# Feed-forward up projection by 7 block products in place of 8, inner tiles in parts of 4, 6, 6, 6

## The reference, cut to what matters

```
def swiglu(x, w_in, w_out):
    gate, up = jnp.split(x @ w_in, 2, axis=-1)
    return (jax.nn.silu(gate) * up) @ w_out
...
h = swiglu(rmsnorm(x, g[0]), lw['ffn_in'][0], lw['ffn_out'][0])
x = x + FFN_RES * rmsnorm(h, g[1])
```

## Time and profile before

| | us |
|---|---|
| median of 3 runs | 2804.49 (2799.52 to 2805.52) |
| the profiled execution, its span | 2804.8 |
| DVE busy | 1252.4 |
| ACT busy | 888.5 |
| POOL busy | 382.5 |

### The profile page before, as it was taken

How to read it: one execution, slowest core, us unless ns; L and a number is a source line. 1 busy time by engine, 2 the same in 40 slices (tenths; PEclk the granted TensorE clock), 3 DMA queues, 4 the chain that set the end, 5 groups by cost and what they waited for, 6 DMA issues and landing times.

```text
span 2804.8 us, 45262 instructions
## 1 busy us (share of the span) xinstructions
PE 2723.6 (97%) x18703; PEld 2610.5 (93%) x18703; DVE 1252.4 (45%) x1697; ACT 888.5 (32%) x1213; POOL 382.5 (14%) x350
## 2 busy tenths in 40 slices
PE   8999999999899999999999999999989999999999
PEld 8999999997679899999999999999966889999998
DVE  4332333647665633333363323345475746332333
ACT  4221123425543422122342212233164533221223
POOL 0110011102143110011101001110022430100110
PEclk9999999999999999999999999999999999999999
DMA  4223223320015222222322222142101152222222
GB/s 131 75 62 89 75 58 88 87 55 10 23 45 93 61 75 71 79 75 58 92 61 75 68 82 75 56 112 69 37 11 32 38 106 66 73 66 82 75 61 81
DMA packets 367939, 191.19 MB, mean 68 GB/s; under 512 B 36477, under 2 KB 363472, under 8 KB 367822
## 3 DMA queue, kind: packets, MB, share of 16 engines
q1 hardware_dynamic: 363822, 179.07, 23.8%
q0 software_dynamic: 4000, 10.47, 1.6%
HBM read 183.58 MB, written 5.93 MB: 68 GB/s over the span
## 4 chain that ended last, share of the span: by engine, by line
PE 88%; DVE 5%; ACT 3%; issue 2%; DMA 1%; SPq 1%; DVEq 0%; ACTq 0%
PE ps L599 25%; PE ps L601 25%; PE ps L600 25%; PE ps L894 2%; DMA raw<-in_w_out_dram 1%; DVE w L1819 1%; PE ps L903 1%; ACT w L1322 1%; PE ps L1022 1%; SPq L510 1%; PE ps L954 1%; DVE at L2117 1%; PE ps L1000 1%; PE ps L1001 0%; DVE mx L2085 0%
## 5 line engine op out<-in xcount | busy, mean ns | idle before, releaser
L599 PE MATMUL ps<-xh,w 128*128 128x320 f32 x3456 | 1076.3, 311 | 24.9 <-DVE xl L1896 13.6
L601 PE MATMUL ps<-xh,w 128*128 128x320 f32 x3456 | 1070.9, 310 | 0.0
L600 PE MATMUL ps<-xl,w 128*128 128x320 f32 x3456 | 1070.9, 310 | 0.0
L599 PEld LDWEIGHTS ps<-xh,w 128*128 128x128 f32 x3456 | 651.3, 188 | 35.1 <-DVE xl L1896 20.6
L600 PEld LDWEIGHTS ps<-xl,w 128*128 128x128 f32 x3456 | 651.6, 189 | 0.3
L601 PEld LDWEIGHTS ps<-xh,w 128*128 128x128 f32 x3456 | 651.5, 189 | 0.0
L1819 DVE TENSOR_TENSOR w<-raw,w 128x2048 fp32r<-128x2048 f32 x172 | 400.3, 2327 | 385.2 <-ACT w L1322 385.1
L1322 ACT ACTIVATE w<-raw 128x2048 fp32r<-128x2048 f32 (+2 forms) x185 | 342.7, 1852 | 435.2 <-PE ps L601 407.0
L599 PE MATMUL ps<-hh,w 128*128 128x320 f32 x1408 | 436.9, 310 | 1.0 <-DVE w L1819 1.0
L601 PE MATMUL ps<-hh,w 128*128 128x320 f32 x1408 | 435.1, 309 | 0.0
L600 PE MATMUL ps<-hl,w 128*128 128x320 f32 x1408 | 435.1, 309 | 0.0
(11 more groups left out here) (367 smaller groups left out, 2657.2 us busy)
## 6 DMA issues: line engine op xcount, KB each, us to landing
raw<-in_w_ffn_in_dram SPq DMA_DIRECT2D x178, 512.0 KB
raw<-in_w_ffn_out_dram SPq DMA_DIRECT2D x64, 384.0 KB
raw<-in_w_ffn_out_dram SPq DMA_DIRECT2D x64, 320.0 KB
raw<-in_w_in_dram SPq DMA_DIRECT2D x38, 512.0 KB
raw<-in_w_out_dram SPq DMA_DIRECT2D x12, 512.0 KB
out_dram<-xio SPq DMA_DIRECT2D x5, 512.0 KB
xin<-in_x_prompt_dram SPq DMA_DIRECT2D x1, 2048.0 KB, 8.1
y<-in_cache_ckv_dram POOLq DMA_DIRECT2D x8, 256.0 KB, 3.3
```

The lines of the kernel that those rows point to most:

```text
L599: pe.matmul(out, wh, xh, start=first, stop=False)
L600: pe.matmul(out, wh, xl, start=False, stop=False)
L601: return pe.matmul(out, wl, xh, start=False, stop=last)
```

## The change

The up projection of one inner tile is a 2 x 2 by 2 x 2 block product: weight blocks are (gate, up) x (first, second half of the contraction), input blocks are (halves of the contraction) x (halves of the tokens). Eight block products of 12 matmuls each are replaced by seven (`PRODUCTS`, the Winograd form of Strassen's scheme), with sums of blocks around them:

- Per unit, GpSimd forms four sums of 128x512 weight blocks (`sums`: s3 = a11 - a21, a21 = a21 + a22, s2, s4) and multiplies `up` by R; ScalarE and VectorE split seven blocks of 128x512 rather than one of 128x2048 (`product_hi`, `product_lo`); the weight buffer is no longer double but seven slots of which each is rewritten when its product is done. Seven small VectorE sums and two ScalarE copies of 128x320 put the products together.
- Per feed-forward block, four sums of input blocks are formed and split once (`g_of_x`, `combined`, `fourth_hi`, `fourth_lo`).
- HH and HL shrink to 6 tiles to make room; the parts are 4, 6, 6, 6. The first part is computed plainly (`plain_up`, 96 matmuls a unit), the other 18 units by 7 products (84 matmuls). There are 4 x 8 down units instead of 2 x 8, with 24 or 36 matmuls.
- In a down stage the first two units are worked together: their last chunk comes after all the others (`chunk`). The split of a down unit's weights now stands behind the eviction (and in the last part behind the square), two units ahead instead of one.

Core of the diff (in the DVE part, `gated` multiplies silu(gate) by up):

```diff
-UP_A, UP_B = 12, 10
+PARTS = (4, 6, 6, 6)
+HT, HMAX = sum(PARTS), max(PARTS)
 DOWN = KD
-FFN_UNITS = UP_A + DOWN + UP_B + DOWN
+PART_AT = [sum(PARTS[:p]) + p * DOWN for p in range(len(PARTS))]
+FFN_UNITS = HT + len(PARTS) * DOWN
...
+QUARTERS = KD // 2
+BLK = QUARTERS * P
+PRODUCTS = ((0, True), (1, True), (2, True), (3, True), (0, False), (3, False), (2, False))
+LASTP = len(PRODUCTS) - 1
+STRASSEN = HT - PARTS[0]
+COPY_P1, COPY_P5 = 0, 1
...
+    def down_w(j, n):
+        at = j * 4096
+        return WF[:, at:at + n * P], WF[:, at + n * P:at + 2 * n * P]
...
+        def strassen_unit(l, u, j, g):
+            pe.wait_ge(drained, u + 1)
+            for s, (bank, fresh) in enumerate(PRODUCTS):
+                if s < LASTP:
+                    pe.wait_ge(*pl_sb.nth(l, LASTP * g + s))
+                else:
+                    pe.wait_ge(lo_ready, u + 3)
+                if s == 4:
+                    pe.wait_ge(*pc_sb.nth(l, 2 * g + COPY_P1))
+                if s == 5:
+                    pe.wait_ge(*pu_sb.nth(l, 4 * g + SUM_57))
+                if s == 6:
+                    pe.wait_ge(*pc_sb.nth(l, 2 * g + COPY_P5))
+                for k in range(QUARTERS):
+                    xh, xl = product_x(s, k)
+                    mm = three(PS[:, 4 * j + bank, 0:HALF], slot_hi(s, k), slot_lo(s, k), xh, xl,
+                               fresh and k == 0, k == QUARTERS - 1, True)
+                mm.then_inc(unit_done if s == LASTP else pd_ps.sem, 1)
...
+            for j in range(2):
+                begin(unit(l, base, 0, j))
+                for k in range(n - 1):
+                    if j == 0:
                         pe.wait_ge(*hl_ready.nth(l, h_from + k))
-                    mm = halves(j, 4 * j, k, n, P, 0, HH, HL, None)
-                mm.then_inc(unit_done, 1)
-
+                    chunk(j, k)
+            pe.wait_ge(*hl_ready.nth(l, h_from + n - 1))
             for j in range(2):
-                narrow_unit(0, j, j == 0)
+                chunk(j, n - 1).then_inc(unit_done, 1)
...
+        def product_hi(l, at, q, g, s):
+            j = q % 2
+            if s in (1, 2, 3, LASTP):
+                act.wait_ge(*ss_sb.nth(l, 4 * g + {1: 2, 2: 1, 3: 0, LASTP: 3}[s]))
+            elif s == 0:
+                act.wait_ge(loaded[j], turn(l, at, q // 2, 0))
+            if q == 0:
+                act.wait_ge(unit_done, unit(l, at, 0, 0) + (1 if s < 4 else 2))
+            elif s < LASTP:
+                act.wait_ge(*pd_ps.nth(l, LASTP * (g - 1) + s))
+            else:
+                act.wait_ge(unit_done, unit(l, at, 0, q - 1) + 3)
+            run(slot_hi(s), slot_raw(s, j), ACT.Copy).then_inc(hi_ready if s == LASTP else ph_sb.sem, 1)
...
+        def plain_up(l, f, base):
+            n, h0 = PARTS[0], f * HT
+            for k in range(n):
+                if k == 2:
+                    split_hi(l, base, 1, 1)
+                if k == 3:
+                    split_hi_d(l, base + n, 0, 0, n)
+                silu(l, k % 2, h0 + k)
+                high_h(l, k % 2, h0 + k, k)
+                if k:
+                    for c in (2 * k - 2, 2 * k - 1)[0:2] if k < 3 else ():
+                        act.wait_ge(*xc_dve.nth(l, f * n_x + XC_SUM[c]))
+                        run(TC[:, 0, :, c, :], T123[c % 2], ACT.Copy).then_inc(xc_act.sem, 1)
+            split_hi_d(l, base + n, 0, 1, n)
...
+            with act.Fori(0, DOWN // 2 - 1) as i:
                 for j in range(2):
-                    step(0, j, False)
-            with act.Fori(1 if first else 0, pairs) as i:
-                for j in range(2):
-                    step(i, j, True)
-
-        def down(l, base, stage=None):
-            with act.Fori(0, DOWN // 2 if stage is None else DOWN // 2 - 1) as i:
-                for j in range(2):
-                    split_hi(l, base, i, j + 1)
                     if stage is not None:
                         square_y(l, i, j, unit(l, base, i, j), stage)
+                    split_hi_d(l, base, i, j + 2, n)
...
+        def strassen_up(l, f, p, base):
+            at, n = base + PART_AT[p], PARTS[p]
+            h0 = f * HT + sum(PARTS[:p])
+            def gated_up(q):
+                dve.wait_ge(*upr_sb.nth(l, strassen(f, p, q)))
+                gated(l, q % 2, h0 + q)
+            for q in range(n):
+                j, g, u = q % 2, strassen(f, p, q), unit(l, at, 0, q)
+                more = q + 1 < n
+                a, b, c, d = (PS[:, 4 * j + bank, 0:HALF] for bank in range(4))
+                if more:
+                    product_lo(l, at, q + 1, g + 1, 0)
+                if q:
+                    gated_up(q - 1)
+                dve.wait_ge(*pc_sb.nth(l, 2 * g + COPY_P1))
+                dve.wait_ge(*pd_ps.nth(l, LASTP * g + 1))
+                V.tensor_tensor(GB[:, j, N2], b, GB[:, j, N2], ALU.add).then_inc(pu_sb.sem, 1)
+                if more:
+                    product_lo(l, at, q + 1, g + 1, 1)
+                    product_lo(l, at, q + 1, g + 1, 2)
+                else:
+                    split_lo_d(l, at + n, 0, 0, n)
+                dve.wait_ge(*pc_sb.nth(l, 2 * g + COPY_P5))
+                dve.wait_ge(*pd_ps.nth(l, LASTP * g + 3))
+                V.tensor_tensor(UB[:, j, N2], d, UB[:, j, N2], ALU.add).then_inc(pu_sb.sem, 1)
+                if more:
+                    product_lo(l, at, q + 1, g + 1, 3)
+                dve.wait_ge(*pu_sb.nth(l, 4 * g + SUM_16))
+                dve.wait_ge(*pu_sb.nth(l, 4 * g + SUM_57))
+                V.tensor_tensor(UB[:, j, N2], GB[:, j, N2], UB[:, j, N2], ALU.add)
+                dve.wait_ge(*pd_ps.nth(l, LASTP * g + 4))
+                V.tensor_tensor(GB[:, j, N1], a, R[:, N1], ALU.mult).then_inc(pu_sb.sem, 1)
+                if more:
+                    product_lo(l, at, q + 1, g + 1, 4)
+                dve.wait_ge(*pd_ps.nth(l, LASTP * g + 5))
+                V.tensor_tensor(UB[:, j, N1], d, GB[:, j, N2], ALU.add).then_inc(pu_sb.sem, 1)
+                if more:
+                    product_lo(l, at, q + 1, g + 1, 5)
+                dve.wait_ge(unit_done, u + 3)
+                V.tensor_tensor(GB[:, j, N2], c, GB[:, j, N2], ALU.add).then_inc(drained, 1)
+                dve.wait_ge(drained, u + 3)
+                V.tensor_tensor(GB[:, j, N2], GB[:, j, N2], R[:, N2], ALU.mult).then_inc(gate_ready.sem, 1)
+                if more:
+                    product_lo(l, at, q + 1, g + 1, LASTP)
+                else:
+                    split_lo_d(l, at + n, 0, 1, n)
+            gated_up(n - 1)
...
+        def plain_up(l, f, base):
+            n, h0 = PARTS[0], f * HT
+            for k in range(n):
+                j, u = k % 2, unit(l, base, 0, k)
+                if k == 2:
+                    split_lo(l, base, 1, 1)
+                if k == 3:
+                    split_lo_d(l, base + n, 0, 0, n)
                 dve.wait_ge(unit_done, u + 3)
                 V.tensor_tensor(two(GB[:, j, :]), PS[:, 4 * j:4 * j + 2, 0:HALF], two(R[:, :]), ALU.mult)\
                     .then_inc(gate_ready.sem, 1)
-                dve.wait_ge(*hl_ready.nth(l, 2 * i + (h0 + j - 2)))
+                dve.wait_ge(*hl_ready.nth(l, h0 + k - 2))
                 V.tensor_tensor(two(UB[:, j, :]), PS[:, 4 * j + 2:4 * j + 4, 0:HALF], two(R[:, :]), ALU.mult)\
                     .then_inc(drained, 1)
                 dve.wait_ge(drained, u + 3)
-                dve.wait_ge(*silu_ready.nth(l, 2 * i + (h0 + j)))
-                V.tensor_tensor(UB[:, j, :], GB[:, j, :], UB[:, j, :], ALU.mult).then_inc(h_ready.sem, 1)
-
-            if first:
-                for j in range(2):
-                    step(0, j, False)
-            with dve.Fori(1 if first else 0, pairs) as i:
-                for j in range(2):
-                    step(i, j, True)
-
-        def down(l, base, add):
-            def step(i, j):
-                split_lo(l, base, i, j + 1)
+                gated(l, j, h0 + k)
+                if k in (1, 2):
+                    for c in (2 * k - 2, 2 * k - 1):
+                        combined(l, f, c)
+                    for c in (2 * k - 2, 2 * k - 1):
+                        combined_lo(l, f, c)
+            split_lo_d(l, base + n, 0, 1, n)
...
+            with dve.Fori(0, DOWN // 2 - 1) as i:
                 for j in range(2):
-                    step(i, j)
-            if add:
-                i = DOWN // 2 - 1
-                step(i, 0)
+                    evicted(i, j)
+                    split_lo_d(l, base, i, j + 2, n)
+            i = DOWN // 2 - 1
+            evicted(i, 0)
+            if stage is not None:
                 split_lo(l, base, i, 2)
+                return
+            for s in range(4):
+                after(s)
+            evicted(i, 1)
+            for s in range(4, len(PRODUCTS)):
+                after(s)
...
+        def sums(l, at, q, g, fourth):
+            a11, a12, a21, a22 = (RAW[:, q % 2, b * BLK:(b + 1) * BLK] for b in range(4))
```

(92 more changed lines are left out.)

257 lines of the change are left out of this document (182 added, 75 removed).

## The result

The kernel after takes 2919.7 us (median of 4 runs, 2913.5 to 2924.6) against 2805.0 for the kernel before: a ratio of 1.0413, 95% interval 1.0398 to 1.0427. That is 115 us slower. I had forecast 2846 with a range up to 2900: right in sign, wrong in size.

A forecast was written before the change was run, and what follows sets the result against it. It took TensorE's number of matmuls to bound the feed-forward blocks, other engines hidden. Against the profiled 2804.8 us it summed -126.7 + 102 + 23 + 13 + 14 + 16 = +41 to 2846 us, slower; range 2755 to 2900.

The forecast's parts named there:

- the turns: In up units, VectorE operations with two SBUF inputs alternate with GpSimd's, so TensorE waits before product 6: +102 us.
- (d): Part 1 to part 2: weight load, sums and split make product 2 late, next sums meet remaining splits: +16 us.
- 864 matmuls: In 18 of 22 up units of four blocks, 12 matmuls each are removed, all on the path: -126.7 us.
- (a): Down stages: unit 3 waits for its freed buffer to be copied and split, after the square in the last part: +23 us.
- (b): Part 1 to its down stage: unit 2's weights queue behind the last h's high part, 3.3 us a block: +13 us.
- (c): Unit 3 of each block: its split comes late behind input copies and sums, by 3.1 to 4.5 us: +14 us.
- forecast cycle: Middle up units: VectorE's list between two sums into ub takes 14.7 us against TensorE's 12.32; four long intervals a part.
- Rival 1: Up units: turns don't bite because GpSimd's work falls into VectorE's pauses; units under 12.6 us, total 2718; chance 0.18.
- rival 2: Up units: GpSimd's sums cost 1.04 us, so a unit takes 13.7 us; total 2798, no clear change; chance 0.15.
- rival 3: Up units: the page's full hold makes each turn 0.15 us longer, 15.6 us a unit; total 2889; chance 0.11.
- granted clock 1.00: Sign listed for a right forecast: TensorE's granted clock stays at 1.00 despite the new stops.
- a rival of its own: Rival 4: TensorE's clock falls at the new stops, 48 at 1.4 us each, +67, some 2915; chance 0.06.

The follow-up runs named there:

- `f1_fit`: The kernel after with idle matmuls put ahead of the waits where TensorE stops, their number fitted to each stop (5 to 29): 2886.9 us, ratio 1.0294.

## Why the prediction was wrong

Its steps against the measured terms (stops start to start: the printed idle time plus 0.165 us each). Of the 52 stops before product 6, 94.3 + 52 x 0.165 = 103 us, 48 are the turns; the other four, 2.62 us idle each, are in the first unit of part 2, so they belong to (d), which had foreseen that the next sums meet the remaining splits:

| Term | Forecast | In the profile after |
|---|---|---|
| 864 matmuls | -126.7 | -126.7 |
| turns, 12 parts (48 stops) | +102 | +92 |
| (a) third down unit, (b) part 1 to down | +36 | 36.0 + 20 x 0.165 = +39 |
| (c) unit 3's split | +14 | 22.0 - 9.2 [before: all stops on such splits] = +13 |
| (d) part 1 to part 2 | +16 | 10.9 + 8 x 0.165 = +12, and 4 x 2.8 before product 6 = +11 |
| not foreseen: last units' squares (L706) | 0 | +5 |
| not foreseen: other intervals below 0.6 us | 0 | +7 |
| TensorE's clock | 0 | +62 |

**The mechanism held.** A VectorE operation with two inputs in SBUF and a GpSimd operation take turns; the splits read from PSUM show it by themselves. By the rule of the Trainium skill, page SBUF — State Buffer, section Who interferes with whom, a VectorE instruction with at most one SBUF input doesn't contend, and the splits that read PSUM agree (0.686 us against 1.07). The forecast cycle was 14.7 us with four long intervals; it is 14.4, with a longer first one. Rivals 1 and 2 are out, and so is rival 3: 14.4 is on the other side of 14.7 from its 15.6. (Rival 1's sum took 40 us for the stage changes, where the forecast and rival 2 took 66; with 66 it would have been 2744.)

**The stage terms held** in (a) to (c) to 3 us, and each of these waits stood where it was put: 3.60 us before unit 3, 3.01 before part 1's second down unit, 1.13 before the third, 2.90 in the last part. (d) was too small by 7. Putting two steps elsewhere gave back 35 us. That all stops together come to 172 us against 168 forecast is partly luck: the turns were 10 us below their term, (d) and the last units' squares 12 above theirs, and the slow clock hid some of the waiting. In `f1_fit`, where the clock is held up, the stops come to 193 us, of which 112 are the turns.

**The failed step is "granted clock 1.00".** The forecast adds up the stops and prices the clock at nothing; I gave the clock 0.06 as a rival of its own instead of a term beside the others. The runs show 62 us of half pace in its place, of which 33 come off the time when the clock is held up. Without them the kernel takes 2887, inside my range; the 41 us from there to 2846 are mostly stops, 193 us at full clock against the 168 forecast, and 10 us of half pace that the fill left. Row had shown it: a stop of 2.4 us, and then 0.83. The rival's price, 67, is what the account shows (62), but by luck, for its rule was wrong: 48 stops at 1.4 each. The trace has 42 half-level stretches against 6 before. One of 3.4 us costs 1.5 (12.8 matmuls at 0.267 us instead of 0.147, 0.12 each), ten are twice as long, and nearly every stop of 2.75 us or more brought one: these are in the second units of the parts and at the stage changes. Of the stops of some 1.8 us in mid-part under half did.

**What stays open.** The two terms that nobody foresaw, 12 us, weren't taken apart, nor was the reason why a part's first interval is longer than the rest. And I can't show why, of two equal 2.12 us stops, one brings the clock down and the next doesn't. The Trainium skill, page TensorE: Matmul & The Clock Gate, section Part 1: The HAM clock gate (the "warmup" mystery), says that the window in which TensorE's activity is watched runs freely and isn't reset when a kernel starts. By that, where a stop falls would matter. The two windows don't contradict it, but no run here moved a stop against it.
